# Where the residual update between stages is done: on GpSimd and VectorE, or on VectorE alone

## What is computed

```
def rms_norm(x, g, eps=NORM_EPS):
    xf = x.astype(jnp.float32)
    y = xf * lax.rsqrt(jnp.mean(xf * xf, axis=-1, keepdims=True) + eps)
    return (y * g.astype(jnp.float32)).astype(x.dtype)
...
        h = h + rms_norm(m, mix_post_g[i])
        u = rms_norm(h, mlp_pre_g[i])
        h = h + rms_norm(sq_relu_mlp(u, w_mlp_up[i], w_mlp_down[i]), mlp_post_g[i])
        e = p[i] @ w_ple_proj[i]
        gate = jax.nn.sigmoid(h @ w_ple_gate[i])
        h = h + rms_norm(e * gate, ple_post_g[i])
```

## Time and profile before

| | us |
|---|---|
| median of 3 runs | 2676.54 |
| lowest, highest | 2671.68, 2677.91 |
| the profiled execution's own time | 2678.17 |
| its span in the profile | 2676.4 |

### The profile page before, as it was taken

The page is one execution under the profiler, slowest core; times in us unless marked ns, Lnnn a source line. Parts: engine busy times, 40 slices in busy tenths (PEclk is TensorE's granted clock), DMA queues, the critical chain, the costliest instruction groups (busy, mean ns, idle before and its releaser), DMA issues.

```text
span 2676.4 us, 33969 instructions
## 1 busy us (share of the span) xinstructions
PE 2532.7 (95%) x14359; PEld 2089.0 (78%) x14359; DVE 1433.8 (54%) x1447; ACT 1085.0 (41%) x1169; POOL 254.4 (10%) x237
## 2 busy tenths in 40 slices
PE   8999989989999999999898998998999999999897
PEld 6887768768888878878676976777888888888775
DVE  4566764655544445445545567646544444444554
ACT  4455420444434334334344444544434334334332
POOL 3001343030000000000122001012000000000121
PEclk9999999889999999999998999998999999999998
DMA  8556402346565555555543654255565565555542
GB/s 265 185 177 205 138 26 98 127 158 231 182 197 188 187 173 182 193 182 176 173 157 100 195 173 149 75 199 191 177 197 193 182 197 188 187 190 184 177 146 74
DMA packets 224820, 453.22 MB, mean 169 GB/s; under 512 B 7834, under 2 KB 16344, under 8 KB 223404
## 3 DMA queue, kind: packets, MB, share of 16 engines
q1 hardware_dynamic: 218816, 430.11, 49.4%
q0 software_dynamic: 3648, 17.54, 1.9%
q10 hardware_dynamic: 2219, 3.59, 0.5%
HBM read 445.52 MB, written 2.10 MB: 167 GB/s over the span
## 4 chain that ended last, share of the span: by engine, by line
PE 86%; DVE 7%; ACT 3%; issue 2%; ACTq 1%; DMA 0%; SPq 0%; DVEq 0%
PE psum L294 26%; PE psum L296 25%; PE psum L295 25%; DVE wlo L276 2%; ACT whi L272 1%; DVE h L437 1%; PE psum L592 1%; PE psum L708 1%; PE psum L318 1%; PE psum L1500 1%; PE psum L1481 1%; PE psum L1496 1%; ACT junk L382 0%; PE psum L839 0%; ACTq L1050 0%
## 5 line engine op out<-in xcount | busy, mean ns | idle before, releaser
L276 DVE TENSOR_TENSOR wlo<-raw,whi 128x2048 fp32r<-128x2048 f32 (+1 forms) x406 | 934.7, 2302 | 1050.9 <-ACT whi L272 1050.6
L272 ACT ACTIVATE whi<-raw 128x2048 fp32r<-128x2048 f32 (+1 forms) x408 | 774.9, 1900 | 1212.0 <-PE psum L296 1186.1
L294 PE MATMUL psum<-whi,uTh 128*128 128x512 f32 (+2 forms) x2176 | 856.7, 394 | 8.3 <-DVE wlo L276 3.5
L295 PE MATMUL psum<-wlo,uTh 128*128 128x512 f32 (+2 forms) x2176 | 845.1, 388 | 6.9 <-issue 6.9
L296 PE MATMUL psum<-whi,uTl 128*128 128x512 f32 (+2 forms) x2176 | 845.1, 388 | 0.0
L294 PEld LDWEIGHTS psum<-whi,uTh 128*128 128x128 f32 x2176 | 411.8, 189 | 98.2 <-issue 11.8
L295 PEld LDWEIGHTS psum<-wlo,uTh 128*128 128x128 f32 x2176 | 411.9, 189 | 87.7 <-issue 9.4
L296 PEld LDWEIGHTS psum<-whi,uTl 128*128 128x128 f32 x2176 | 411.2, 189 | 82.4
L294 PE MATMUL psum<-whi,hTh 128*128 128x512 f32 x1024 | 400.6, 391 | 6.1 <-DVE wlo L276 6.1
L296 PE MATMUL psum<-whi,hTl 128*128 128x512 f32 x1024 | 398.6, 389 | 0.0
L295 PE MATMUL psum<-wlo,hTh 128*128 128x512 f32 x1024 | 398.5, 389 | 0.0
(11 more groups left out here) (354 smaller groups left out, 1562.2 us busy)
## 6 DMA issues: line engine op xcount, KB each, us to landing
raw<-in_w_mlp_up SPq DMA_DIRECT2D x128, 1024.0 KB, 5.2
raw<-in_w_mlp_down SPq DMA_DIRECT2D x128, 1024.0 KB, 5.1
raw<-in_ab_w_in SPq DMA_DIRECT2D x48, 1024.0 KB, 5.2
raw<-in_w_ple_gate SPq DMA_DIRECT2D x32, 1024.0 KB, 5.1
raw<-in_c_w_in SPq DMA_DIRECT2D x24, 1024.0 KB, 5.3
raw<-in_ab_w_out SPq DMA_DIRECT2D x16, 1024.0 KB, 5.1
raw<-in_c_w_out SPq DMA_DIRECT2D x16, 1024.0 KB, 5.0
raw<-in_c_w_in SPq DMA_DIRECT2D x12, 736.0 KB, 4.4
```

What stands on the lines that cost most here:

```text
L272: act.activation(whi[:, q % 2, :, 0:n], raw[:, q, :, 0:n], ACT.Copy).then_inc(hi_ready, 1)
L276: dve.tensor_tensor(wlo[:, q % 2, :, 0:n], raw[:, q, :, 0:n], whi[:, q % 2, :, 0:n].bitcast(F32), ALU.subtract).then_inc(lo_ready, 1)
L294: pe.matmul(o, xh, hi, start=(q == 0 and k == 0), stop=False)
L295: pe.matmul(o, xh, lo, start=False, stop=False)
```

## The change

The marks `h_late` and `m_late` go, `h_ready` now counts all eight pieces of h, and a new buffer `mg` takes block 3 of m times `gpost`.

- GpSimd (`h_gain_pool`) keeps only the multiplication of m by `gpost` for blocks 0, 1 and 2: six instructions a boundary.
- VectorE (`m_last`) multiplies block 3 by `gpost` into `mg`, two instructions ahead of rstd. For that it waits for the stage's last product: `m_out` after a mixer, else its own last instruction on m.
- VectorE does all eight pieces of the update, block 3 from `mg`. Blocks 2 and 3 stand behind `split_lo` 1 and behind `T_dve` 1 in `h_first`; at the end all four blocks follow one another.

```
+    def m_last(dve, link, st, prev):
+
+        dve.wait_ge(*mark("gpost", prev, 16))
+        if prev.endswith("_out"):
+            dve.wait_ge(*mark("m_out", prev, 4))
+        elif prev.startswith("mlp"):
+            dve.wait_ge(*mark("ev_dn", prev, 16))
+        else:
+            dve.wait_ge(*mark("gated", prev, 4))
+        for tt in range(TT):
+            dve.tensor_tensor(mg[:, tt, :], m[:, tt, 3 * W:4 * W], gpost[:, 3 * W:4 * W],
+                              ALU.mult).then_inc(sem("m_last"), 1)
+
     def h_update(dve, link, st, prev, b):
 
         if b == 0:
+            m_last(dve, link, st, prev)
             dve.wait_ge(*mark("m_sq", prev, 8))
             rstd_from(dve, link, ssq[:], rstd_m[:], D, NORM_EPS).then_inc(sem("rstd_m"), 1)
             dve.wait_ge(*mark("rstd_m", st, 1))
...
+        if b < 3:
+            dve.wait_ge(*mark("m_gained", st, 2 * b + 2))
+        else:
+            dve.wait_ge(*mark("m_last", st, 2))
         for tt in range(TT):
...
+            x = m[:, tt, b * W:(b + 1) * W] if b < 3 else mg[:, tt, :]
+            dve.scalar_tensor_tensor(out=h_src(tt, b), in0=x, scalar=rstd_m[:, tt:tt + 1], in1=h_src(tt, b),
+                                     op0=ALU.mult, op1=ALU.add).then_inc(sem("h_ready"), 1)
...
-        pool.wait_ge(*mark("rstd_m", st, 1))
-        if prev == "ab_out":
-            pool.wait_ge(sem("x_back"), 64)
-        for b in range(late(st), 4):
-            for tt in range(TT):
-                mb, i = m[:, tt, b * W:(b + 1) * W], 2 * (b - late(st)) + tt + 1
-                pool.wait_ge(*mark("m_gained", st, 2 * b + tt + 1))
-                pool.tensor_tensor(mb, mb, rstd_m[:, tt:tt + 1].broadcast_to([P, W]),
-                                   ALU.mult).then_inc(sem("m_late"), 1)
-                pool.wait_ge(*mark("m_late", st, i))
-                pool.tensor_tensor(h_src(tt, b), h_src(tt, b), mb, ALU.add).then_inc(sem("h_late"), 1)
...
         T_dve(dve, st, 0, gain)
         split_lo(dve, s, 1, n)
+        if prev:
+            h_update(dve, link, st, prev, 2)
         T_dve(dve, st, 1, gain)
+        if prev:
+            h_update(dve, link, st, prev, 3)
         for b in (2, 3):
```

More of the change, by code:

```diff
@@ L152, in build @@
     gate = at("gate", [P, TT, W], F32, 144)
+    mg = at("mg", [P, TT, W], F32, 148)
     za = at("za", [P, TT, A_IN], F32, 120)
@@ L237, in build @@
               "m_out": lambda st: 4 if st.endswith("_out") else 0,
-              "h_ready": lambda st: 4 if updates(st) else 0, "h_late": lambda st: 4 if updates(st) else 0,
-              "m_gained": lambda st: 8 if updates(st) else 0, "m_late": lambda st: 4 if updates(st) else 0, "rstd_m": lambda st: 1 if updates(st) else 0,
+              "h_ready": lambda st: 8 if updates(st) else 0, "m_last": lambda st: 2 if updates(st) else 0,
+              "m_gained": lambda st: 6 if updates(st) else 0, "rstd_m": lambda st: 1 if updates(st) else 0,
               "gpost": lambda st: 0 if st.endswith("_in") else 16,
@@ L392, in h_squares @@
         return squares
-    def late(st):
-        return 3 if st == "end" else 2
     def h_ready(st):
-        return lambda tt, b: ((sem(f"x_in{b}"), 16) if st == order[0] else
-                              mark("h_ready", st, 2 * b + tt + 1) if b < late(st) else
-                              mark("h_late", st, 2 * (b - late(st)) + tt + 1))
+        return lambda tt, b: ((sem(f"x_in{b}"), 16) if st == order[0] else mark("h_ready", st, 2 * b + tt + 1))
     def rsqrt(dve, link, x):
@@ L430, in h_update, with h_gain_pool @@
             dve.wait_ge(*mark("rstd_m", st, 1))
-        dve.wait_ge(*mark("m_gained", st, 2 * b + 2))
-        if b == 0 and prev == "ab_out":
-            dve.wait_ge(sem("x_back"), 64)
+            if prev == "ab_out":
+                dve.wait_ge(sem("x_back"), 64)
+        if b < 3:
+            dve.wait_ge(*mark("m_gained", st, 2 * b + 2))
+        else:
+            dve.wait_ge(*mark("m_last", st, 2))
         for tt in range(TT):
-            dve.scalar_tensor_tensor(out=h_src(tt, b), in0=m[:, tt, b * W:(b + 1) * W], scalar=rstd_m[:, tt:tt + 1],
-                                     in1=h_src(tt, b), op0=ALU.mult, op1=ALU.add).then_inc(sem("h_ready"), 1)
-    def h_update_pool(pool, st, prev):
+            x = m[:, tt, b * W:(b + 1) * W] if b < 3 else mg[:, tt, :]
+            dve.scalar_tensor_tensor(out=h_src(tt, b), in0=x, scalar=rstd_m[:, tt:tt + 1], in1=h_src(tt, b),
+                                     op0=ALU.mult, op1=ALU.add).then_inc(sem("h_ready"), 1)
+    def h_gain_pool(pool, st, prev):
         pool.wait_ge(*mark("gpost", prev, 16))
-        for b in range(4):
+        for b in range(3):
             pool.wait_ge(*mark("m_sq", prev, 2 * b + 2))
@@ L2330, in _ @@
             if updates(st) and prv[st]:
-                h_update_pool(pool, st, prv[st])
+                h_gain_pool(pool, st, prv[st])
             if st == "c_in":
@@ L2339, in _ @@
                 pool.dma_start(gpost[:], g.partition_broadcast(P)).then_inc(sem("gpost"), 16)
-        h_update_pool(pool, "end", end)
+        h_gain_pool(pool, "end", end)
     @block.scalar
@@ L2390, in _ @@
                 out_dve(dve, link, st)
-        for b in range(late("end")):
+        for b in range(4):
             h_update(dve, link, "end", end, b)
```

## The result

The changed kernel takes 2642.36 us (four runs, 2638.78 to 2646.57) against 2676.06 (four runs) for the kernel before: ratio 0.9877, 95% interval 0.9858 to 0.9896, so 33.7 us faster. Measured again beside the later experiments it took 2643.78 against 2674.83, ratio 0.988 (0.986 to 0.990), 31 us. The forecast was 2647.5, 29 us, with a range of 2640 to 2657. The profiled execution took 2641.49, with a span of 2639.7.

What follows compares the result with a forecast made beforehand. TensorE (86% of the chain) was taken as the bound, waiting at stage boundaries. Savings of 10.1 (PLE), 5.5 (MLPs), 5.0 (c_in) and 5.4 (end) make 26 us, plus 3 for the clock, 29: 2647.5 us, range 2640 to 2657.

Steps and rivals of the forecast that it cites:

- rstd loses 2.0 us: At all six boundaries, rstd's two slow instructions (1.14 and 1.19 us) lose their excess once GpSimd stops at block 2.
- The updates take 0.65 us each: First four updates of h at a boundary: 2.65 us in place of 6.43, without GpSimd working beside VectorE.
- The first matmul at R + 4.85 and R + 5.05: Microseconds after R, the end of rstd: 4.85 into ple0, nearly tied with TensorE's transposes (4.7); 5.05 into MLPs and c_in.
- The multiplications: VectorE's pair on block 3: 1.3 us, fitting into ScalarE's squares; after a mixer, R comes 0.3 us later.
- Updates 2 and 3 hidden: 1.3 us each in VectorE's queue, costed at nothing; margin 1 us in the MLPs, 0.2 us in c_in.
- Rival 2: VectorE's queue limits quarters 1 and 2; TensorE waits 1 to 2 us at five boundaries, 8 in all: 2655; chance 0.07.
- The end: Kernel's end: rstd done 2.0 us earlier, eight updates in 5.35 us, four stores from 2664.1 to 2670.1; saves 5.4 us.
- The clock, mis-sized: Cold first-quarter matmuls lose 7.9 us before; forecast gain 3 us, bounds a gain of 7.9 and a loss of 3.3.
- counting from unbroken work: Clock rises 4.6 us after unbroken TensorE work begins; first-quarter matmuls cold 1.3 us, losing 3.3 in place of 7.9.
- counted from the first transposes: Rival at the first quarters: clock rises no sooner, 11.2 us lost in place of 7.9, total 2654; chance 0.15.
- Rival 3: VectorE's slow pace is its own; the four updates stay at 6.4 us, kernel 7 us slower, 2683.5; chance 0.03.
- Rival 4: GpSimd's block 2 multiplications slip into the boundary; gain partly lost, time within 0.2% or a little faster; chance 0.02.

Runs made afterwards that it cites:

- The first of the isolating runs: Kernel before, GpSimd's updates of blocks 2 and 3 held until VectorE has done blocks 0 and 1, except at the end: 2653.50 and 2652.39 us.
- the second: Kernel before with only block 3's multiplication moved to VectorE ahead of rstd, GpSimd still updating blocks 2 and 3: 2667.39 us, ratio 0.9979.
- The all-first run: Changed kernel with the updates of blocks 2 and 3 also ahead of block 0's low parts: 2654.66 us, ratio 0.9939.
- the last run: Changed kernel with VectorE's block 3 multiplication later after the mixers, and 5 to 7 throwaway matmuls a boundary: 2630.05 us, ratio 0.9838.

## Why the prediction was right, point by point

- **rstd loses 2.0 us.** It takes 2.53 us at every boundary in place of 4.51 to 4.57. The first of the isolating runs shows it stay while the updates shrink, and the second shows the reverse.
- **The updates take 0.65 us each.** 2.74 us for four by the profile's way of counting, 2.65 forecast. Shown by holding GpSimd back.
- **The first matmul at R + 4.85 and R + 5.05.** Measured 4.80, 4.80 and 5.11, 5.10, 5.10. Followed step by step through four engines, this chain was the part that could most easily have gone wrong; the near-tie with TensorE's transposes came out as forecast.
- **The multiplications.** 1.29 us a pair, 1.3 forecast; hidden by the squares where I said, and after a mixer 2.25 us on the path, with R later by 0.2 (0.3 forecast). Stage by stage: 5.1 us into each PLE stage (5.1 forecast, called 10.1 for both), 2.8 into each MLP (2.75), 5.0 into c_in (5.0), 5.6 at the end (5.4). In all 26.4, 26 forecast. Two products of the forecast are off in the last digit without weight for it: 2 × 5.1 is 10.2, and 5 × 2.2, in the bound of the clock, is 11.0.
- **Updates 2 and 3 hidden.** Into c_in, where the margin was to be 0.2 us, block 1's low parts are done in time and block 2's transposes follow quarter 0 without a wait (4.11 us at clock 1.00). Rival 2 didn't come about.
- **The end.** It is now set by the stores, which run back to back behind the blocks of h (DMA share 0.95 from 2633 on); the term was 0.2 us short.
- **The clock, mis-sized.** I took 3 us of the 4.6 that counting from unbroken work gave; the first quarters gave 5.8. By the granted clocks 3.3 us of them were cold, a loss of 1.6, in place of 15.7 and 7.9: 6.2 us. My forecast of a granted clock of 0.85 to 0.95 was met or passed (0.88 to 1.00). The Trainium skill's rule (TensorE: Matmul & The Clock Gate, Part 1), counted from the first transposes, would have lost 3 us more, and I gave it 0.15. The runs decide against that count: the first quarters are shorter. The all-first run tells what I hadn't weighed: a pause between transposes and matmuls matters. How long it may be isn't shown: 2.10 us took the clock back there, while in the last run, where TensorE had been kept busy, 1.02 us ahead of the first matmul of mlp0 left it at 1.00. The kernel before had pauses of 1.20 and 1.14 us among its transposes.
- **Rival 3**, VectorE's own pace, is excluded by the first experiment. **Rival 4**, an overlap left over, didn't come about: GpSimd is idle through every boundary.

The total was 29 us; the two comparisons say 34 and 31. Of what the forecast missed, 2.8 us are the clock and 0.4 the rest of the sum; the remainder is within the runs' spread.

## What to carry to other kernels

Work given to GpSimd is not free for VectorE even when no data are shared: look in the timeline for VectorE instructions that last as long as a GpSimd one beside them, first of all for small ones, and keep GpSimd idle, or merely held back, where VectorE is on the path. On such a path put there only what the next engine waits for, and the rest into the queue where it waits for others anyway. Where TensorE has to wait, bridge the wait with throwaway matmuls sized from their own measured length, so that they end before the data come: that gained 3.3 us here, and too many of them lost 13.4 at the same places. And compare kernels stage by stage, since TensorE's unexplained pauses of some 10 us went with the program and not with the stage that was edited.

## What was not expected of the hardware

- A GpSimd instruction with one input holds VectorE too: four copies of 0.57 us made four VectorE instructions of 0.52 us out of four of 0.16. Each GpSimd instruction held exactly one of VectorE's, of two numbers a partition as of 512, and not every kind: `uTl<-psum,uTh`, with one input in PSUM, took 1.40 us for four beside a working GpSimd and 1.41 without.
- VectorE holds GpSimd as well. In the kernel before `split_lo` (2.3 us alone) ran beside GpSimd's update, and GpSimd's product of m and rstd, 1.04 us long at 1335.15, took 3.09:

```profile
1342.78 3.15 DVE L276 TENSOR_TENSOR wlo<-raw,whi 128x2048 fp32r<-128x2048 f32 x1
```
```profile
1343.74 3.09 POOL L458 TENSOR_TENSOR m<-m,rstd_m 128x512 f32<-128x512 f32 x1
```

- TensorE at 2.4 GHz fell back to 1.2 (matmuls of 0.40 us, then 0.63) within its first few matmuls after a pause of 2.10 us that followed 3.20 us of transposes.
- A float32 matmul of 128x512 stands in the trace as two rows and takes 0.87 us at full clock, against 0.23 us from one matmul to the next for the split numbers of the main product.
